# Norms ahead of a layer taken by halves: half squares, scaling on two engines, first products on half a turned tile, output stored by halves

## The reference

```python
def rmsnorm(x, g):
    xf = x.astype(jnp.float32)
    y = xf * lax.rsqrt(jnp.mean(xf * xf, axis=-1, keepdims=True) + NORM_EPS)
    return (y * g.astype(jnp.float32)).astype(x.dtype)

for i in range(DEPTH):
    h = rmsnorm(x, norm_mix[i])
    # m = mla_mixer(h) for i = 0, 3; moba_mixer(h) for i = 1; ssd_mixer(h) for i = 2
    x = x + m.astype(x.dtype)
    x = x + sq_relu_mlp(rmsnorm(x, norm_mlp[i]), mlp_w1[i], mlp_w2[i]).astype(x.dtype)
return rmsnorm(x, norm_final)
```

## Time and profile before

| | before |
|---|---|
| runs: median (lowest to highest) | 1367.55 us (1367.45 to 1368.42), 3 runs |
| the profiled execution: its own time | 1368.97 us |
| its span | 1367.1 us |
| mean granted TensorE clock, share of full speed | 0.981 |
| PE busy | 1322.6 us, 97% |
| PE weight loads busy | 1201.4 us, 88% |
| DVE busy | 854.2 us, 62% |
| ACT busy | 664.6 us, 49% |
| POOL busy | 40.3 us, 3% |
| DMA, mean | 169 GB/s |

### The profile page before, as it was taken

The page is one execution under the profiler, slowest core; times in us unless marked ns, Lnnn a source line. Parts: engine busy times, 40 slices in busy tenths (PEclk is TensorE's granted clock), DMA queues, the critical chain, the costliest instruction groups (busy, mean ns, idle before and its releaser), DMA issues.

```text
span 1367.1 us, 20299 instructions
## 1 busy us (share of the span) xinstructions
PE 1322.6 (97%) x8600; PEld 1201.4 (88%) x8600; DVE 854.2 (62%) x1125; ACT 664.6 (49%) x834; POOL 40.3 (3%) x58
## 2 busy tenths in 40 slices
PE   5999999999999999998998999999999999999997
PEld 5888899999899899997997988999988888899996
DVE  4777665554655665555897786655556776665553
ACT  4555454444455554443766554544434555554442
POOL 2000000000000000000101110000000000000000
PEclk9899999999999999999998999999998999999999
DMA  8654285555655475553873444755535243475540
GB/s 246 158 159 137 93 270 192 190 192 157 182 173 181 132 244 185 185 158 104 254 226 105 134 158 133 246 187 188 187 117 180 83 136 121 169 245 185 185 154 31
DMA packets 147834, 231.06 MB, mean 169 GB/s; under 512 B 7651, under 2 KB 116493, under 8 KB 147744
## 3 DMA queue, kind: packets, MB, share of 16 engines
q1 hardware_dynamic: 144896, 221.66, 49.3%
q0 software_dynamic: 2848, 8.10, 2.8%
HBM read 227.08 MB, written 2.65 MB: 168 GB/s over the span
## 4 chain that ended last, share of the span: by engine, by line
PE 88%; DVE 6%; ACT 2%; DMA 2%; issue 1%; POOL 0%; SPq 0%; DVEq 0%; POOLq 0%; ACTq 0%
PE bank L521 16%; PE bank L523 15%; PE bank L522 15%; PE acc L726 11%; PE acc L727 11%; PE acc L730 11%; DVE wlo L504 2%; PE bank L1125 1%; PE bank L897 1%; DMA raw<-in_mla_w_in 1%; PE bank L1131 1%; DMA raw<-in_mla_w_ukv 1%; ACT whi L494 1%; PE bank L882 1%; PE bank L650 1%
## 5 line engine op out<-in xcount | busy, mean ns | idle before, releaser
L504 DVE TENSOR_TENSOR wlo<-raw,whi 128x2048 fp32r<-128x2048 f32 (+1 forms) x209 | 467.7, 2245 | 194.3 <-ACT whi L494 194.3
L494 ACT ACTIVATE whi<-raw 128x2048 fp32r<-128x2048 f32 (+1 forms) x209 | 389.1, 1871 | 92.3 <-PE acc L730 79.1
L521 PE MATMUL bank<-hhi,whi 128*128 128x256 f32 x1448 | 414.8, 286 | 5.3 <-DVE xn L1690 3.2
L522 PE MATMUL bank<-hlo,whi 128*128 128x256 f32 x1448 | 411.5, 284 | 0.0
L523 PE MATMUL bank<-hhi,wlo 128*128 128x256 f32 x1448 | 411.5, 284 | 0.0
L521 PEld LDWEIGHTS bank<-hhi,whi 128*128 128x128 f32 x1448 | 278.7, 192 | 11.0 <-issue 6.9
L522 PEld LDWEIGHTS bank<-hlo,whi 128*128 128x128 f32 x1448 | 278.7, 192 | 3.3 <-issue 1.0
L523 PEld LDWEIGHTS bank<-hhi,wlo 128*128 128x128 f32 x1448 | 278.6, 192 | 0.2
L727 PE MATMUL acc<-wlo,uhi 128*128 128x512 f32 x512 | 200.0, 391 | 0.0
L726 PE MATMUL acc<-whi,uhi 128*128 128x512 f32 x512 | 199.6, 390 | 0.0
L730 PE MATMUL acc<-whi,ulo 128*128 128x512 f32 x512 | 159.1, 389 | 0.0
(11 more groups left out here) (214 smaller groups left out, 1633.2 us busy)
## 6 DMA issues: line engine op xcount, KB each, us to landing
raw<-in_mlp_w SPq DMA_DIRECT2D x128, 1024.0 KB, 5.3
raw<-in_ssd_w_in SPq DMA_DIRECT2D x18, 1024.0 KB, 6.0
raw<-in_mla_w_o SPq DMA_DIRECT2D x16, 1024.0 KB, 5.1
raw<-in_mla_w_ukv SPq DMA_DIRECT2D x8, 1024.0 KB, 6.4
raw<-in_moba_w_qkv SPq DMA_DIRECT2D x16, 512.0 KB, 7.4
raw<-in_ssd_w_out SPq DMA_DIRECT2D x8, 1024.0 KB, 5.0
raw<-in_mla_w_uq SPq DMA_DIRECT2D x8, 768.0 KB, 8.8
raw<-in_mla_w_in SPq DMA_DIRECT2D x4, 1024.0 KB, 7.8
```

Of the source, the lines that this page charges most:

```text
L494: nc.scalar.activation(whi[:, s, :e], raw[:, s, :e], ACT.Copy).then_inc(w_hi_done[s], 1)
L504: nc.vector.tensor_tensor(wlo[:, s, :e], raw[:, s, :e], whi[:, s, :e].bitcast(F32), ALU.subtract).then_inc(w_split[s], 1)
L521: nc.tensor.matmul(ps, lhs[0], rhs[0], start=start, stop=False)
L522: nc.tensor.matmul(ps, lhs[0], rhs[1], start=False, stop=False)
```

## The change

It touches four norms: those ahead of MoBA (`j` = 2), SSD (`j` = 4) and the second MLA (`j` = 6), and the final one (`j` = 8). The first norm and the deferred ones keep their code.

- ACT squares each half of x as soon as it is there, into two sums (`act_sumsq_halves`, with 1/1024 folded into the scale); DVE adds the two sums and epsilon in one instruction (`dve_scale_lower`).
- DVE multiplies the upper half of x by the gain ahead of `rstd` (`dve_gain_upper`); when `rstd` is there DVE makes the lower half of xn as before and ACT multiplies the upper half by `rstd` in place (`act_scale_upper`).
- In MLA and MoBA the first products wait for the half of the turned tile that they read, at k = 0 and k = 4. In SSD the wait for the upper half of tile 0 is moved behind the products of the lower half, and the transposes of tile 1's lower half are put ahead of the wait for tile 0.
- In SSD and the final norm ACT squares tile 1 ahead of copying the turned tile 0, and DVE scales tile 1 ahead of the low parts of tile 0.
- The output is stored in four DMAs of 256 KB, each waiting for its half.

Declarations of the new tile `ssq_half` (two sums for each norm and tile) and of the semaphores `xg_done` and `xn_upper_done`, and the same hook `ready_at(k)` in `pe_moba_v`, are left out here:

```diff
...
@@ -543,6 +546,28 @@
             nc.scalar.activation(junk[:], x[:, t, :], ACT.Square,
                                  accum_out=ssq[:, j * T + t:j * T + t + 1]).then_inc(ssq_done, 1)
 
+        def fast(j):
+
+
+            return j > 0 and not deferred(j)
+
+        def act_sumsq_halves(act, j, t):
+            c = j * T + t
+            act.wait_ge(ssq_done, c)
+            for half in range(2):
+                n = slice(512 * half, 512 * half + 512)
+                act.wait_ge(x_ready, (j - 1) * 2 * T + 2 * t + half + 1)
+                ins = nc.scalar.activation(junk[:, n], x[:, t, n], ACT.Square, scale=DM ** -0.5,
+                                           accum_out=ssq_half[:, c, half:half + 1])
+            ins.then_inc(ssq_done, 1)
+
+        def act_scale_upper(act, j, t):
+            act.wait_ge(xg_done, norm_index[j] * T + t - T + 1)
+            act.wait_ge(rstd_done, norm_index[j] * T + t + 1)
+            n = slice(512, 1024)
+            nc.scalar.activation(xn[:, t, n], xn[:, t, n], ACT.Copy,
+                                 scale=rstd[:, j * T + t:j * T + t + 1]).then_inc(xn_upper_done, 1)
+
         def act_tr(act, j, t):
             for half in range(2):
                 ps = job_ready(act, ("tr", j, t, half))
...
@@ -550,6 +575,20 @@
                                      ps[:].rearrange("p (k n) -> p k n", k=4), ACT.Copy).then_inc(h_hi_done, 1)
 
         def act_norm(act, j):
+            if fast(j):
+                scan = j < len(stages) and stages[j][0] == "ssd"
+                act_sumsq_halves(act, j, 0)
+                act_scale_upper(act, j, 0)
+                if j == len(stages) or scan:
+                    act_sumsq_halves(act, j, 1)
+                if j < len(stages):
+                    act_tr(act, j, 0)
+                    if not scan:
+                        act_sumsq_halves(act, j, 1)
+                act_scale_upper(act, j, 1)
+                if j < len(stages):
+                    act_tr(act, j, 1)
+                return
             for t in range(T):
                 if not deferred(j):
                     act_sumsq(act, j, t)
...
@@ -588,6 +627,22 @@
                 nc.vector.scalar_tensor_tensor(out=xn[:, t, n], in0=x[:, t, n], scalar=rstd[:, c:c + 1],
                                                in1=gbc[:, n], op0=ALU.mult, op1=ALU.mult).then_inc(xn_done, 1)
 
+        def dve_gain_upper(dve, j, t):
+            dve.wait_ge(gain_loaded, 16 * (j + 1))
+            wait_x(dve, j, t)
+            n = slice(512, 1024)
+            nc.vector.tensor_tensor(xn[:, t, n], x[:, t, n], gbc[:, n], ALU.mult).then_inc(xg_done, 1)
+
+        def dve_scale_lower(dve, j, t):
+            c = j * T + t
+            n = slice(0, 512)
+            dve.wait_ge(ssq_done, c + 1)
+            nc.vector.scalar_tensor_tensor(out=ms[:, c:c + 1], in0=ssq_half[:, c, 0:1], scalar=EPS,
+                                           in1=ssq_half[:, c, 1:2], op0=ALU.add, op1=ALU.add).then_inc(ms_done, 1)
+            dve.wait_ge(rstd_done, norm_index[j] * T + t + 1)
+            nc.vector.scalar_tensor_tensor(out=xn[:, t, n], in0=x[:, t, n], scalar=rstd[:, c:c + 1], in1=gbc[:, n],
+                                           op0=ALU.mult, op1=ALU.mult).then_inc(xn_done, 2)
+
         def dve_tr(dve, j, t, halves=(0, 1)):
             for half in halves:
                 dve.wait_ge(h_hi_done, j * 4 + 2 * t + half + 1)
...
@@ -599,6 +654,24 @@
         def dve_norm(dve, j):
 
 
+            if fast(j):
+                dve_residual(dve, j - 1, 0)
+                dve_gain_upper(dve, j, 0)
+                dve_scale_lower(dve, j, 0)
+                dve_residual(dve, j - 1, 1)
+                dve_gain_upper(dve, j, 1)
+                if j == len(stages):
+                    dve_scale_lower(dve, j, 1)
+                elif stages[j][0] == "ssd":
+                    dve_scale_lower(dve, j, 1)
+                    for half in range(2):
+                        dve_tr(dve, j, 0, [half])
+                        dve_tr(dve, j, 1, [half])
+                else:
+                    dve_tr(dve, j, 0)
+                    dve_scale_lower(dve, j, 1)
+                    dve_tr(dve, j, 1)
+                return
             if j:
                 dve_residual(dve, j - 1, 0)
             dve_scale_x(dve, j, 0)
...
@@ -615,13 +688,6 @@
                 dve_residual(dve, j - 1, 1, [1])
                 dve_scale_half(dve, j, 1, 1)
                 dve_tr(dve, j, 1, [1])
-            else:
-                dve_residual(dve, j - 1, 1)
-                if j < len(stages):
-                    dve_tr(dve, j, 0)
-                dve_scale_x(dve, j, 1)
-                if j < len(stages):
-                    dve_tr(dve, j, 1)
 
         def dve_square_rstd(dve, j):
 
...
@@ -643,7 +709,10 @@
         def pe_tr(te, j, t, halves=(0, 1)):
 
             for half in halves:
-                te.wait_ge(xn_done, 2 * (j * T + t) + half + 1)
+                if fast(j) and half:
+                    te.wait_ge(xn_upper_done, norm_index[j] * T + t - T + 1)
+                else:
+                    te.wait_ge(xn_done, 2 * (j * T + t) + half + 1)
                 ps = open_job(te, ("tr", j, t, half))
                 for k in range(4):
                     kk = 4 * half + k
...
@@ -658,12 +727,13 @@
         def pe_first_two(te, j, products):
 
 
-            tile_ready(te, j, 0)
-            products(0, 0)
+            def ready_by_halves(t):
+                return lambda k: tile_ready(te, j, t, [2 * k // KD]) if k in (0, KD // 2) else None
+
+            products(0, 0, ready_by_halves(0))
             pe_tr(te, j, 1)
             products(1, 0)
-            tile_ready(te, j, 1)
-            products(0, 1)
+            products(0, 1, ready_by_halves(1))
             products(1, 1)
 
         def pe_channels(te, ps, key, width, parts=None):
...
@@ -683,8 +753,8 @@
             if deferred(j):
                 tile_ready(te, j, 0)
             else:
-                tile_ready(te, j, 0)
                 pe_tr(te, j, 1, [0])
+                tile_ready(te, j, 0, [0])
             tile_ready(te, j, 1, [0])
             half = KD // 2
 
...
@@ -711,6 +781,7 @@
                     pe_tr(te, j, 1, [1])
                 if items[6:]:
                     part(key, items[6:], False)
+            tile_ready(te, j, 0, [1])
             tile_ready(te, j, 1, [1])
             part(keys[0], products(keys[0], (0, 1), upper_k), True).then_inc(used(keys[0])[0], 1)
             key = keys[1]
...
@@ -1073,13 +1144,14 @@
         def pe_mla(te, j, L):
             M = mla_sems[L]
 
-            def compress(n, t):
+            def compress(n, t, ready_at=lambda k: None):
                 key = (("cq", "ckv")[n], L)
                 if t == 0:
                     wait_unit(te, key)
                 ps = open_job(te, ("c", L, t)) if n == 0 else bank[jobs.at["c", L, t][0]]
                 w = hi_lo(key)
                 for k in range(KD):
+                    ready_at(k)
                     mm = mm3(ps[:, n * 256:(n + 1) * 256], (hhi[:, k, tok(t)], hlo[:, k, tok(t)]),
                              (w[0][:, k, :], w[1][:, k, :]), k == 0, k == KD - 1)
                 if t == 1:
...
@@ -1843,9 +1916,14 @@
                     dst = raw[:, s, :a * b].rearrange("p (a b) -> p a b", a=a)[:, :, i * w:(i + 1) * w]
                     sp.dma_start(dst, src).then_inc(raw_loaded[s], 16)
             for t in range(T):
-                sp.wait_ge(xn_done, 2 * ((NN - 1) * T + t + 1))
-                sp.dma_start(out[0, t * P:(t + 1) * P, :], xn[:, t, :]).then_inc(out_stored, 16)
-            sp.wait_ge(out_stored, 16 * T)
+                for half in range(2):
+                    if half:
+                        sp.wait_ge(xn_upper_done, norm_index[NN - 1] * T + t - T + 1)
+                    else:
+                        sp.wait_ge(xn_done, 2 * ((NN - 1) * T + t + 1))
+                    n = slice(512 * half, 512 * half + 512)
+                    sp.dma_start(out[0, t * P:(t + 1) * P, n], xn[:, t, n]).then_inc(out_stored, 16)
+            sp.wait_ge(out_stored, 32 * T)
 
         @block.gpsimd
         def _(pool):
...
```

More of the change, by code:

```diff
@@ L131, in build @@
         neghalf = sb("neghalf", [P, 4])
+        ssq_half = sb("ssq_half", [P, NN * T, 2])
         acc = [[ctx.enter_context(nc.psum_tensor(f"acc{t}{h}", [P, 512], F32)) for h in range(2)] for t in range(T)]
@@ L150, in build @@
         xn_done = sem("xn_done")
+        xg_done = sem("xg_done")
+        xn_upper_done = sem("xn_upper_done")
         pool_const = sem("pool_const")
@@ L1244, in pool_mla, with pe_moba_v @@
                                         ALU.pow).then_inc(M["c_rstd_done"], 1)
-        def pe_moba_v(te, L, p, t):
+        def pe_moba_v(te, L, p, t, ready_at=lambda k: None):
             key = ("mv", L, p)
@@ L1288, in pe_moba @@
         def pe_moba(te, j, L):
-            pe_first_two(te, j, lambda n, t: pe_moba_v(te, L, n, t))
```

(1 more changed line is left out.)

## The result

The changed kernel took 1370.58 us (median of 10 runs, 1369.25 to 1372.48), the kernel before, beside it on the same chip, 1367.48 us (10 runs, 1365.89 to 1371.11). The ratio is 1.0022 [1.0013, 1.0032]: slower by 0.2%, about 3 us, where 4.65 us less had been forecast. The profiled execution took 1370.93 us, its span 1369.1 us at a mean granted clock of 0.987; before it was 1367.1 us at 0.981.

A forecast was written before the change was run, and what follows sets the result against it. PE was taken to bound the kernel (88% of the span), norms mattering only where PE waits. 1.0 + 1.0 + 1.05 + 1.1 = 4.15, + 0.5 for the clock: 4.65 us, median 1362.9 us, range 1360.3 to 1366.2.

The forecast's parts named there:

- Nothing behind the norms gives it back, as far as the trace shows: After the norms: all engines start a stage's work from the same event, all earlier, so the 4.65 us saved stays.
- 4.15: All four changed norms and the store, without the clock: 1.0 + 1.0 + 1.05 + 1.1 us saved.
- MoBA and MLA: Norms ahead of both: 0.4 us from half squares, 0.6 from one DVE instruction less; 1.0 us saved in each.
- the closing list: Signs to check: mean 0.9 us behind the residual, PE pauses near 1.5 us, SSD waits 2.6 and 1.4, store issue 3.6.
- ACT's upper scaling: In MoBA and MLA: 0.74 us on ACT, as long as DVE's own half, covered since PE turns the lower half first.
- Rival 4: Per-row scaling on ACT needs another function table; loads of 1.28 us make the kernel 5.6 us slower, 1373.2; chance 0.03.
- Rival 3: In MoBA and MLA the change does not do what it says: 3.5 us saved, 3.0 without the clock, 1364.3; chance 0.12.
- SSD: Norm ahead of SSD: ACT squares tile 1 first, so xn comes at 644.25 instead of 645.25; 1.05 us saved.
- The end: Final norm and store by halves: last store lands near 1365.5 instead of 1366.6; 1.1 us saved (0.75 to 1.4).
- The clock: +0.5: Behind shorter PE pauses: 0.9 us lost instead of 1.5 at MoBA and MLA, nearly no change at SSD; +0.5 us taken.
- the 3.9 us of slow stretches: Low clock behind the pauses: 1.5 us lost at MoBA, 2.4 at SSD; +3.9 if the clock falls in none.

The follow-up runs named there:

- e1: The kernel before with an unused tile of 160 bytes where the change has its new one, so all tiles behind move 160 bytes: 1378.3 us, 1.0077.
- e13: The changed kernel with 96 unused bytes behind its new tile, so the tiles behind it move by 256 bytes in all: 1361.88 us, 0.9961.
- e14: The kernel before with 256 unused bytes in the place of the new tile, moving all tiles behind by 256: 1367.21 us, 0.9992.
- e12: The changed kernel at distance 192, but first products of MoBA and MLA wait for the whole turned tile: 1365.56 us, 0.998.
- e11: The changed kernel at distance 192, with only the final norm and the store changed, keeping the changed order of PE's waits: 1365.03 us, 0.9976.
- e5: The kernel before with `raw`, `whi` and `wlo` moved 32 bytes and all else 64: 1364.77 us, 0.9979.
- e9: The kernel before with `hhi` and `hlo` moved 32 bytes and the tiles behind them 64: 1365.66 us, 0.9979.
- e18: The kernel before with `hhi` and `hlo` 128 bytes from `whi` and `wlo`, the rest moved by 256: 1367.83 us, 0.9996.

## Why the prediction was wrong

**The step that failed** is the sentence "Nothing behind the norms gives it back, as far as the trace shows", and with it the part-by-part cost, in which the new tile had no term. Its price is the +10.5 us of e1 (0.77%). e13 against the change as it stands gives 1.0022 - 0.9961 = 0.6%, 8.3 us. The 2.2 us between these two prices I can't assign. The granted clock is one candidate: the changed kernel's ten runs have 0.985 to 0.988, e13's 0.982 to 0.985, and in the kernel before 0.003 went with 2.2 us. But e1 too ran a little higher (0.983) than the kernel before (0.981), so the account stays open. None of my rivals held this: the slower one was a table load in ACT, and it did not come. The trace of before could not have priced the step, as all its distances were 0, but the diff shows a new tile ahead of others, and a range should have said so.

The length of each stretch, from the start of one stage's transposes to the next's (the first from the start, the last to the end of the span), from the timelines of PE:

```
stretch ends at:  MLP0    MoBA    MLP1    SSD     MLP2    MLA     MLP3    end
before           164.88  185.09  107.10  184.48  200.78  185.25  147.40  192.12
e1               163.92  186.79  107.40  186.46  201.81  186.96  148.76  194.00
after            165.98  186.43  105.37  186.45  200.80  186.66  144.52  192.89
e14              163.83  185.07  105.60  184.45  200.63  185.25  147.38  192.09
e13              164.84  184.67  105.20  184.47  199.64  184.83  145.39  190.96
```

e1 loses 1.7 to 2.0 us in each of the four MLPs (the columns MoBA, SSD, MLA and end), the columns in which the changed kernel loses 0.8 to 2.0. From e14 to e13, both with distance 0, the stretches behind the first shrink by 0.4, 0.4, 0, 1.0, 0.4, 2.0 and 1.1: 5.3 us. The gains stand where the changed norms are, but the 2.0 us in MLA (the column MLP3) are not the norm's alone. Some 16 us behind MLA's transposes lies a slow stretch that no row of the prediction covers; over the 28 us around it e14 was granted 0.76 and e13 0.82, which makes 1.7 us. First e14, then e13:

```profile
1037.00:1065.00 28.00, 27.02 (x174) 25.58 (x173) 16.01 (x33) 10.82 (x17) 1.35 (x2) 0.76 0.53 196
```

```profile
1036.00:1064.00 28.00, 27.02 (x181) 25.24 (x180) 18.06 (x41) 12.54 (x23) 1.35 (x2) 0.82 0.51 187
```

The first stretch has the same code in both (between 163.7 and 166.8 in all runs) and is 1.0 us longer in e13. Both profiles have the same mean granted clock, 0.984, and their spans differ by 4.3 us: 4.15 had been forecast for the norms. That the medians' 5.3 lies close to the whole forecast of 4.65 is in part luck.

**MoBA and MLA: right, a little too much.** From the mean to the end of the second residual half it was to be 0.9 us; 350.56 less 349.77, the end of the residual, is 0.79. From that end to the first product it is 355.11 - 349.77 = 5.34 us against 353.20 - 347.01 = 6.19: 0.85 us saved, 1.0 forecast. The rest is small waits: DVE waits 0.09 us for its own residual before each gain product, and the lower scaling starts 0.93 us after the mean, not 0.85. PE's pause was to be 1.6 us (1.5 in the closing list): 1.66, 1.62, and 1.72 in e13's timeline of MLA:

```profile
1023.65 1.09 PE L720 MATMUL bank<-ident,xn 128*128 128x128 f32 x8
1026.46 0.36 PE L525 MATMUL bank<-whi,hhi 128*128 128x256 f32 x1 [1.72 <-DVE hlo L650]
```

**ACT's upper scaling: right.** The group in the changed kernel has 723 ns where 0.74 us was worked out, and the table loads by line are as long as before, with none at L568:

```profile
L560 ACT ACTIVATE junk<-x 128x512 f32<-128x512 f32 x16 | 10.0, 628 | 20.0 <-DVE x L851 20.0
...
L568 ACT ACTIVATE xn<-xn,rstd 128x512 f32<-128x512 f32 x8 | 5.8, 723 | 6.6 <-POOL rstd L703 6.6
L1603 ACT ACT_TABLE_LOAD x4 | 5.1, 1283 | 2.8 <-DVE dec L1704 2.8
```

Rival 4 falls with this. Rival 3 falls too: a half square is shorter on the path, and e12 shows that the half-tile waits bring 0.6 us a stage.

**SSD: right.** Waits of 2.6 and 1.4 us forecast, 2.40 and 1.46 measured. From the last matmul's end to the first product: 649.78 - 644.39 = 5.4 us, against 648.30 - 641.71 = 6.6 before: 1.2 saved, 1.05 forecast.

**The end: right.** From the last matmul's end to the end of the span 7.5 us before, 6.3 after and in e13: 1.2 saved, 1.1 forecast. The issue of the last store begins 3.7 us behind the last matmul, 3.6 forecast. The scalings of the last tile, in the timeline after, begin together:

```profile
1362.41 0.39 PE L801 MATMUL acc<-whi,ulo 128*128 128x512 f32 x1
...
1365.27 0.72 ACT L568 ACTIVATE xn<-xn,rstd 128x512 f32<-128x512 f32 x1 [0.92 <-POOL rstd L703]
1365.28 0.75 DVE L643 SCALAR_TENSOR_TENSOR xn<-x,rstd,gbc 128x512 f32<-128x512 f32 x1 [0.74 <-POOL rstd L703]
```

A store of 256 KB landed in 2.2 us, one of 512 KB in 2.6. The prediction's 1.1 us took the two stores' data one behind the other, 0.65 us each; the rows give 0.4 us for the data that a half has less. The page "DMA: Bandwidth & Descriptors" of the Trainium skill, section "Anatomy of one DMA — SWDGE (gpsimd) path", gives 2.0 us and the bytes at 436 GB/s, which makes, as an estimate, 2.6 us for a half and 3.2 for the whole; the stores here are issued by SP, not by gpsimd, and both land sooner. The 0.3 us that the prediction took for a half's data by that page is 0.6 by the page's own rate.

**The clock: +0.5 can't be confirmed.** The windows (us; PE, PEld, DVE, ACT, POOL; PEclk; DMA; GB/s) behind the pauses of the changed kernel, against the earlier trace rows:

```profile
355.10:358.30 3.20, 3.19 (x27) 3.20 (x28) 1.28 (x3) 0.97 (x3) 2.36 (x3) 1.00 0.35 26
649.80:655.30 5.50, 5.50 (x35) 5.02 (x36) 1.31 (x4) 1.99 (x2) 0.00 (x0) 0.70 1.02 319
```

No fall at MoBA where it was 0.54, and a shorter one at SSD: the direction forecast. But e14, whose code is that of before and whose pauses are 0.48 and 1.90 us, kept 1.00 at MoBA as well, in the like window of its trace:

```profile
352.10:355.30 3.20, 3.18 (x27) 3.20 (x28) 1.57 (x3) 0.00 (x0) 2.36 (x3) 1.00 0.30 31
```

So whether that pause lets the clock fall changes from run to run with the pause unchanged, and one profile can't say what the shorter pause did. With 4.15 for the norms, e13's 5.3 leaves about 1 us to the clock and chance; +0.5 was forecast, and the interval of e13 (3.4 to 7.2 us) can't tell them apart. At the same median clock of 0.984 e13 lies 5.3 us below e14 and 4.7 below the kernel before's 18 runs, so the norms alone gave about what was forecast for them or a little more. The slow stretch inside MLA, which cost e14 6.7 us (28 us at 0.76), weighs more than the 3.9 us of slow stretches that the prediction priced, and in e11 it was gone without any change of the norm ahead of it.

## What to carry to other kernels

A new tile, however small, is an edit to every tile declared behind it: compare the addresses before and after, and either declare it last or pad it until the operand pairs of the matmuls lie as before (here to 256 bytes; a `pad` of 96 bytes turned 0.2% slower into 0.4% faster). When a local gain arrives and the total does not, compare the mean durations and the step from one to the next of the commonest instruction in both traces, also in lines the change doesn't touch: 5.8 ns on 2304 matmuls outweighed four norms. And placement can be tuned for its own sake: moving two tiles by 32 bytes gave 0.9% on the old kernel, and 1.3% together with the change.

## What the runs showed of the hardware

The pace of these matmuls depends on where their operand tiles lie in a partition, and ordered by the distance of the two, modulo 256 bytes, the runs make one table. Over 512 columns distance 0 is best (227.5 ns), 192 nearly so (229), and 32, 64, 128 and 160 cost 5 ns each. Over 256 columns with `hhi` and `hlo` distance 32 is better (116.7 ns) than 0 or 128 (120); with `chi` and `clo` 192 is best (118.3) and 0 worst (124.2).

That the distance is what counts is argued, not shown. For the 512 columns the address of the moved tile alone, modulo 256, orders the runs as well, since only e5 moved `whi`. One reading speaks for the pair: `chi` is moved by 64 bytes in both e5 and e9, and its block took 121.2 ns a matmul in e5, where `whi` had moved too, and 122.1 in e9. One speaks against the distance as the whole of it: the 228.8 ns of e18.

The weight loads don't explain the pace. Those of `whi` ahead of `hhi` took 188 ns in the mean in e5, 193 in the kernel before, but 190 in e18, whose pace is not better; those of `uhi` took 188 before, after and in e5, while the pace went from 227.5 to 233.3. Not tried: 96 and 224, `hhi` and `hlo` at 64, 160 and 192, the absolute address with the distance held (a move of both operands together), and whether writes of ACT and DVE to these tiles take part. Why the widths and the tiles want different distances is open.

A mean granted clock that differs by 0.003 between runs of one kernel goes with 2.2 us here (101 runs of the kernel before), some two fifths of what the whole change is worth. Which slow stretches a run gets is not settled by the length of the pause ahead of them: 0.54 in one run and 1.00 in another behind like pauses of 0.48 and 1.9 us.
